# A decoder layer on one core: projection order, the opening of the mix, and the sums of squares rearranged

## What is computed

```
x = x + 0.5 * swiglu(rmsnorm(x, ffn1_norm), w_gate, w_up, w_down)         # hidden width 2816
h = rmsnorm(x, mix_norm)
sq, sk, sv, gq, gk, gv, gg, glr, mq = split(h @ w_in)                     # 512,128,128,128,128,256,256,16,256
y_swa = swa_attention(sq, sk, sv, ..., sinks, rel_bias)                   # 8 heads, window 128, T5 bias, sinks
y_gla = gla(gq, gk, gv, gg, glr, w_gate_up, b_gate, norm_gain)            # 4 heads, chunked gated linear attention
mk, mv = split(rmsnorm(mem, mem_norm) @ w_mem_kv)
y_mem = memory_attention(mq, mk, mv, ...)                                 # 4 heads over the 256 memory tokens
x = x + concat(y_swa, y_gla, y_mem) @ w_out
x = x + 0.5 * swiglu(rmsnorm(x, ffn2_norm), ...)                          # second feed-forward, the same shape
```

## Time and profile before

| | value |
|---|---|
| three runs | 1735.8, 1737.96, 1741.29 us |
| the profiled execution | 1740.66 us |
| its span, first to last instruction | 1738.8 us |
| TensorE (PE) busy | 1701.1 us, 98% |
| weight loads (PEld) busy | 1385.8 us, 80% |
| VectorE busy | 1128.4 us, 65% |
| ScalarE busy | 717.3 us, 41% |
| GpSimd busy | 530.7 us, 31% |
| mean granted TensorE clock | 0.994 of full |
| transfers | 110 GB/s over the span |

### The profile page before, as it was taken

One profiled execution on the slowest core, in us unless ns is written; L12 is line 12 of the kernel. 1 busy time (PEld: TensorE's weight loads), 2 busy tenths in 40 slices (PEclk: granted clock), 3 DMA queues, 4 the chain that ended last, 5 costly groups with the idle time before them and its releaser, 6 DMA issues.

```text
span 1738.8 us, 24811 instructions
## 1 busy us (share of the span) xinstructions
PE 1701.1 (98%) x8295; PEld 1385.8 (80%) x8295; DVE 1128.4 (65%) x1582; ACT 717.3 (41%) x1350; POOL 530.7 (31%) x432
## 2 busy tenths in 40 slices
PE   7999999999999999999989999999999999999999
PEld 4888888888888789887756678888888888888877
DVE  8975556555498595247868873985555555569654
ACT  5533333333344562142157831443333333334432
POOL 0454455444130141000046612155554444310000
PEclk9999999999999999999989999999999999999999
DMA  7142222333764431120100122222233322584434
GB/s 201 60 164 91 98 95 93 111 122 133 281 213 127 149 91 61 61 73 25 37 1 2 38 98 91 79 85 104 90 105 119 113 103 90 172 290 149 121 109 163
DMA packets 101693, 191.69 MB, mean 110 GB/s; under 512 B 11491, under 2 KB 13972, under 8 KB 101612
## 3 DMA queue, kind: packets, MB, share of 16 engines
q1 hardware_dynamic: 100528, 188.48, 32.2%
q0 software_dynamic: 848, 2.10, 0.9%
q10 hardware_dynamic: 236, 0.06, 0.0%
HBM read 139.74 MB, written 50.86 MB: 110 GB/s over the span
## 4 chain that ended last, share of the span: by engine, by line
PE 94%; DVE 2%; ACT 2%; POOL 1%; DMA 1%; issue 1%; ACTq 0%; DVEq 0%
PE ps L56 29%; PE ps L57 29%; PE ps L58 29%; PE ps L1597 1%; PE ps L1568 1%; PE ps L1549 1%; PE ps L1288 1%; POOL Pg L1935 1%; PE ps L2300 1%; DMA down_raw<-act_dram 1%; ACT glu L1732 0%; PE ps L1646 0%; PE ps L1634 0%; PE ps L1367 0%; DVE p_lo L1218 0%
## 5 line engine op out<-in xcount | busy, mean ns | idle before, releaser
L488 DVE TENSOR_TENSOR ring<-w_raw,ring 128x512 fp32r<-128x512 f32 x240 | 236.0, 998 | 219.1 <-ACT ring L483 218.9
L58 PE MATMUL ps<-hiT,ring 128*128 128x512 f32 x672 | 261.4, 389 | 0.0
L56 PE MATMUL ps<-hiT,ring 128*128 128x512 f32 x672 | 261.4, 389 | 0.0
L57 PE MATMUL ps<-loT,ring 128*128 128x512 f32 x640 | 249.0, 389 | 0.0
L56 PE MATMUL ps<-down_ring 128*128 128x512 f32 x616 | 240.5, 390 | 3.9 <-DVE xT L910 3.9
L57 PE MATMUL ps<-down_ring 128*128 128x512 f32 x616 | 240.3, 390 | 0.0
L58 PE MATMUL ps<-down_ring 128*128 128x512 f32 x616 | 240.2, 390 | 0.0
L56 PE MATMUL ps<-hiB,ring 128*128 128x512 f32 x576 | 224.9, 390 | 0.0
L58 PE MATMUL ps<-hiB,ring 128*128 128x512 f32 x576 | 224.1, 389 | 0.0
L483 ACT ACTIVATE ring<-w_raw 128x512 fp32r<-128x512 f32 x240 | 150.4, 628 | 174.1 <-PE ps L58 163.0
L857 ACT ACTIVATE down_ring<-down_raw 128x512 fp32r<-128x512 f32 x176 | 108.7, 629 | 226.5 <-DMA down_raw<-act_dram 185.5
(11 more groups left out here) (257 smaller groups left out, 3011.7 us busy)
## 6 DMA issues: line engine op xcount, KB each, us to landing
down_raw<-act_dram SPq DMA_DIRECT2D x154, 256.0 KB, 2.6
w_raw<-in_w_gate SPq DMA_DIRECT2D x88, 256.0 KB, 3.0
w_raw<-in_w_up SPq DMA_DIRECT2D x88, 256.0 KB, 3.2
act_dram<-actT SPq DMA_DIRECT2D x88, 256.0 KB, 2.0
act_dram<-act SPq DMA_DIRECT2D x66, 256.0 KB, 2.0
wd<-in_w_down SPq DMA_DIRECT2D x44, 256.0 KB, 4.9
wd_mirrored<-in_w_down SPq DMA_DIRECT2D x33, 256.0 KB, 4.6
p_raw<-in_w_proj SPq DMA_DIRECT2D x15, 512.0 KB, 3.5
```

The source lines that it names most:

```text
L56: nc.tensor.matmul(out, w_hi, x_hi, start=first, stop=False, skip_group_check=resumed)
L57: nc.tensor.matmul(out, w_hi, x_lo, start=False, stop=False, skip_group_check=resumed)
L58: return nc.tensor.matmul(out, w_lo, x_hi, start=False, stop=last, skip_group_check=resumed)
L488: nc.vector.tensor_tensor(ring[:, e % RING, 1, :], op_source(e), ring[:, e % RING, 0, :].bitcast(F32), ALU.subtract).then_inc(op_ready, 1)
```

## The change

It moves work; two things are added and one is removed.

- *Start.* VectorE no longer adds the squares. TensorE sums both halves with eight ones products each, as the squares come (`sum_squares`). Ahead of them stand ten new matmuls (`WARM`), ones by ones with 128 columns, whose result nobody reads. The bias row's product goes between the two sums and its copy on VectorE behind the second pair of operands. In the head's first part, B11, the first two units take turns over the eight feature tiles instead of one behind the other.
- *First pair.* VectorE makes the low parts of operands 5 and 6 of the first full pair ahead of those of T3 (`EARLY`). In SP's order for the first full pair the reloads of quarter 11 come ahead of the stores of B22 and T1 to T4.
- *Down.* The four additions of product P7 go to the start of step 53, one operand earlier. The load of xT's quarter (1, 0) is issued behind activation load 99, not 113.
- *Projection.* glr comes ahead of gk and gq. The sums of mem's squares stand behind group 7, not 5, and their roots and reciprocals move with them. The last two groups use the PSUM banks 6 and 7.
- *Mix opening.* Spans and both first scores of block 0 stand ahead of the last projection group on TensorE, `bias_max`, `gate_edges` and `denominators` ahead of the last take on VectorE. ScalarE and GpSimd enter the mix without waiting for the last take; GpSimd gates k of block 0 into a place of its own (`kg_first`) and scales unit 0 right away. Two buffers change places for it. The level products of block 0 now wait for the last take.

The diff, cut to its core (the four helpers that moved out of `mix_tensor` and `mix_vector` are unchanged but for what is shown):

```diff
-PROJ = ["v", "gv0", "gv1", "gk", "gq", "glr", "mv0", "mv1", "mk0", "mk1", "k",
+PROJ = ["v", "gv0", "gv1", "glr", "gk", "gq", "mv0", "mv1", "mk0", "mk1", "k",
...
             for part_i, r in enumerate(HEAD_PARTS[:4]):
...
+                if f == 0 and r == "B11":
+                    pe.wait_ge(op_ready, b.head_op + 2)
+                    for k in range(KK):
+                        pe.wait_ge(part_ready, part_count(f, r, k))
+                        for u in units[:2]:
+                            mm = split_product(...)
+                    units = units[2:]
...
-            ops(4)
+            ops(*range(4, 4 + 1 + EARLY))
             lo("T3")
...
             def body(i, first, last):
-                if not first:
-                    for r in ("B22", "B21", "T1", "T2", "T3", "T4"):
-                        store_act(sp, f, r, i - 1)
-                if not last:
+                if first:
+                    for x in range(2):
+                        reload_w(sp, f, x, "11", i)
+                for r in ("B22", "T1", "T2", "T3", "T4") if first else ("B22", "B21", "T1", "T2", "T3", "T4"):
+                    store_act(sp, f, r, i - 1)
+                if not first and not last:
...
+                if q == (AT_ONCE + 1) * PAIRS - 2:
+                    n, mh, h, bank = EVICTS["P7"]
+                    for j in range(4):
+                        down_add(dve, f, AT_ONCE, n, mh, h, bank, j)
                 for k in (2 * q + DOWN_RING, 2 * q + DOWN_RING + 1):
                     if k < 2 * DOWN_STEPS:
                         down_op_lo(dve, f, k)
-                    if k == 2 * (AT_ONCE * PAIRS + PAIRS - 2) + DOWN_RING:
-                        n, mh, h, bank = EVICTS["P7"]
-                        for j in range(4):
-                            down_add(dve, f, AT_ONCE, n, mh, h, bank, j)
...
-        X_BEHIND = {21: (0, 0), 55: (0, 1), 79: (1, 1), 113: (1, 0)}
+        X_BEHIND = {21: (0, 0), 55: (0, 1), 79: (1, 1), 99: (1, 0)}
...
+        def proj_bank(i):
+            return i % 4 if i < NG - 2 else 6 + i - (NG - 2)
...
                 wait(pe, proj_taken, i - 3)
+                if i == NG - 2:
+                    pe.wait_ge(diag_taken, 1)
+                if i == NG - 1:
+                    spans_of(pe, 0)
+                    pe.wait_ge(proj_taken, NG - 2)
+                    pe.wait_ge(head_normed, len(normed))
+                    scores(pe, 0, 0)
+                    scores(pe, 1, 0)
...
-                if i == 5:
+                if i == NB - 1:
                     pe.wait_ge(mem_split, 3)
...
+                if i == NG - 1:
+                    dve.wait_ge(bias_landed, 16)
+                    bias_max(dve, 0, 0)
+                    bias_max(dve, 1, 0)
+                    gate_edges(dve, 0)
+                    denominators(dve, 0, 0)
                 dve.wait_ge(proj_ready, i + 1)
...
+            return LEVEL_BANK if (u, n) == (1, 0) else SCORE_BANK[u]
...
-            pe.wait_ge(proj_taken, NG)
-            pe.wait_ge(head_normed, len(normed))
-            scores(0, 0)
-            spans_of(0)
-            scores(1, 0)
             for n in range(NB):
                 mem_scores(n)
+                if n == 0:
+                    pe.wait_ge(proj_taken, NG)
+                    pe.wait_ge(biased, 8)
                 levels(n)
...
-            act.wait_ge(proj_taken, NG)
             gate_decays(0)
             exps(0, 0)
...
+            pool.wait_ge(head_summed, len(normed))
+            gate_k(0)
+            scale(0, 0)
             pool.wait_ge(proj_ready, NG)
...
+            for _ in range(WARM):
+                nc.tensor.matmul(ps[:, BANK_WARM, 0:P], ones[:, :], ones[:, :], start=True, stop=True)
+            def sum_squares(h):
+                for m in range(KT):
+                    pe.wait_ge(x_squared, KT * h + m + 1)
+                    mm = nc.tensor.matmul(ps[:, BANK_NORM + h, :], ones[:, :], squares[h][:, m, :], start=m == 0, stop=m == KT - 1)
+                mm.then_inc(norm_summed, 1)
+            sum_squares(0)
             pe.wait_ge(rel_bias_landed, 32)
...
-            pe.wait_ge(x_summed, KT - 1)
-            nc.tensor.matmul(ps[:, BANK_NORM, :], ones[:, :], squares[0][:, 0, :], start=True, stop=True
-                             ).then_inc(norm_summed, 1)
-            for m in range(KT):
...
+            sum_squares(1)
             ffn_tensor(pe, 0)
```

205 lines of the change are left out of this document (102 added, 103 removed).

## The result

The changed kernel takes 1719.68 us, the median of four executions (1718.08 to 1721.54). The kernel before, measured beside it, takes 1737.81. The ratio is 0.9894, with a 95% interval of 0.9873 to 0.9914: 18.1 us, or 1.1%, faster. The forecast was 1717. The profiled execution took 1718.25, with a span of 1716.5 and a mean granted clock of 0.999.

What follows compares the result with a forecast made beforehand. TensorE was taken to bound the kernel, busy 1701.1 of 1738.8 us. Terms 3.7 + 5.6 + 4.2 + 2.9 + 6.3 = 22.7 us give 1718.0 from the profiled execution, 1715.3 from the median; forecast 1717, range 1711.5 to 1725.

Steps and rivals of the forecast that it cites:

- Start, 3.7: Start of the kernel: feed-forward 1's first product begins at 20.5 rather than 24.16, a gain of 3.7 us.
- First feed-forward, 0: First feed-forward's pairs: reordered low parts and reloads find no gap to close and are costed at nothing.
- Down, 5.6: Down stages: two waits for additions into xT (3.9 us) and a slow-clock stretch (1.7) go, gaining 5.6 us.
- Projection, 7.1: Projection: 4.2 us from moving mem's sums (wait 2.5, slow stretch 1.7) and 2.9 from moving glr (waits 1.1, 1.8).
- Mix opening, 6.3: Opening of the mix: levels come 3.5 us earlier and 2.8 more is gained up to the second block's transposes.
- The 3.5 at the levels: Mix opening: level products come 11.3 us after the last product but one ends, not 14.8, gaining 3.5.
- The 2.8 for the clock: Mix opening: levels to second block's transposes take 17.46 us at full clock instead of 20.26, gaining 2.8.
- The first (the clock not up for the first sum): Rival at the start: first-sum matmuls cost 1.71 us each; 3.7 lost and 1 added, 1722; chance 0.13.
- That of the opening's clock: Rival at the mix opening: clock falls in the new gap or q's gating takes 2.77; 4 us less, 1721; chance 0.12.
- The slower one: Rival in the dense products: TensorE is granted less clock with gaps closed; 1750 at mean clock 0.975; chance 0.02.
- The gate chain: Rival in the projection: VectorE, held in glr's gate chain, makes TensorE wait for a bank; 2.9 us lost, 1720; chance 0.05.
- load 101: Rival in the down stages: the moved xT load makes this activation load too late; 5.6 us lost, 1723; chance 0.04.

Runs made afterwards that it cites:

- the glr: The kernel before with only glr moved ahead of gk and gq; the stretch up to the sums of the heads took 100.57 us instead of 105.37.
- the mem kernel: The kernel before with only mem's sums of squares moved behind group 7, roots and reciprocals too; the stretch up to the heads' sums took 102.64 us, not 105.37.

## Why the prediction came out as it did

**Start, 3.7.** Right in size and steps. The first sum ended at 12.5 (12.3 forecast), the second began at 13.8 (13.6), B11's first part came at 18.35 (18.5), the first product at 20.40 (20.5). Half of it and more is the ten matmuls. That the first sum ran at full clock from its start was in part luck: in four of the seven kernels with this start the clock rose only after it had begun. The cover that I named, the fifth weight operand's, was 2.0 us (1.8 forecast) and held.

**First feed-forward, 0.** Wrong, by 1.87 us. The step that failed is "what hides them is that the operands stand ready ahead of TensorE". I had looked at operands and parts only. A product also waits for the bank that it writes, and the bank was freed by VectorE at 77.9 before, 1.0 us ahead of need. My own numbers said that TensorE gains 3.7 and VectorE's chain 1.1 to 1.4, so any cover under 2.5 us had to break. Every use of VectorE's results in the first pairs should have been put to that test, banks included.

**Down, 5.6.** The mechanism was right (5.94 against the profiled execution), and its size was that of one execution. The term was made of waits of 1.2 and 2.7 and a stretch of 1.7. In the two other profiled executions that had both edits out (the glr and the mem kernel) the longer wait was 1.1, with no lowered stretch, since the xT load took 5.0 and 5.1 us, not 7.1. Over the three executions the gain is 1.4 in the first stage and 2.2 in the second: 3.6. I also wrote the sum as if both edits were needed. Either one is nearly enough at a load of 5.1; at one of 7.1 neither was tried alone.

**Projection, 7.1.** Right: 2.7 and 3.1 of waits, and a lowered stretch of 1.7 behind the 2.5 in 3 of the 4 profiled executions with that wait, 7.1 on average. Wrong was the reading that shorter waits have no such stretch behind them: one of 1.8 had.

**Mix opening, 6.3.** The 3.5 at the levels is right (3.6, always), with q's gating 0.6 longer than the sum has it and the take 0.5 earlier. The 2.8 for the clock is that of an execution with three stretches. The segment averages 141.4 in five executions of the old form and 136.5 in seven of the new: 4.9. Only against an execution with three stretches is it more, up to 6.9.

**The sum.** With these averages it is 3.4 (the start over five executions of the old and seven of the new form) less 1.9, plus 3.6, 7.1 and 4.9: 17.1, beside the measured 18.1. So the miss of 2.7 us against 1717 is the unseen bank (1.9), and terms taken from an execution that lay 2.7 above its median. I had weighed this by going from 1718.0 and 1715.3 to 1717. The part of the 2.7 that is chance in the waits and stretches cannot be won back from the median: the sum should have been cut by it, 20.0 for 22.7, when it was set against 1738. The low end of the range has a slip as well: the high ends of the parts (4.3, 5.9, 7.3 and 7) add up to 24.5, which from the median gives 1713.5, not 1711.5. The measured 1719.7 lies inside either way.

**Rivals.** The first (the clock not up for the first sum) did not come at its price: in all seven executions the first sum took 7.13 to 7.69 us, against 9.16 without the ten matmuls and the 13.7 of the rival. A small part of it, up to 0.56 us, came in four of the seven. That of the opening's clock came true in 2 of 7, and its other condition, a slower gating of q, by 0.6 of the 1.7 us. The slower one (less clock in dense products) did not happen: 0.999 is above 0.994. The gate chain shows no wait of TensorE, nor does load 101, for which ScalarE alone waited.

## What to carry to other kernels

When a start or a stage is shortened, go on from there and compare how much earlier each engine gets to its next tasks. Where one gains 3.7 us and its feeder 1.1, every cover below the difference breaks, and buffers and banks that are waited for count as covers like operands. A wait or a lowered stretch read from one execution is a sample: take those that depend on a transfer's time or on the clock's fall at a discount, or look at a second execution. Where the same instruction has two durations, see what was already running beside it when it began. Of two edits that cure the same wait, test one alone before counting both.

## What was not expected of the hardware

- The same code at the same place is granted a different clock in different executions: behind the mix's old opening 1.7 us were lost in two profiled executions and 5.1 in three, and behind the wait of 2.5 us in the projection 1.7 in three and nothing in one. At the start it rises at 4.3 to 6.8 us with the same ten matmuls ahead. The granted clock and the time go together: the changed kernel's executions near 1718.1 have a mean clock of 0.999, those near 1721.3 have 0.997, and 0.002 of 1719 is 3.4.
- Behind sixteen matmuls of one column, while TensorE counted as busy, the clock fell in 9 of 12 profiled executions, and in neither of the 2 where they were 128 columns wide. The width cost 0.1 us for the sixteen (3.73 for 3.63).
- VectorE's gating of q (two inputs in SBUF) ended 0.95 us after the GpSimd instruction that it found running, 14 times of 14, and took 1.06 to 1.09 when it found none. Which of the two begins first decides who pays: k's gating took 2.09 ahead of q's and 2.99 behind it.
- One xT load took 7.1 us in one execution and 5.0 to 5.1 in three others, at the same place of the same queue.
- The list of waits named an operand's low part where a bank was waited for. Only the end times beside the wait, 0.1 us apart, told the two apart.
